# A hybrid decoder step on one core: the turns of the sample's next keys as a stream of their own, and the attention's order planned anew

## The chip, the cores and the metric
One core of a Trainium2 chip. The time is device microseconds of one launch of the whole step, measured from the device's side.

## The reference, cut to what matters
One layer of a decoder for two groups of tokens that share the weights: a prompt of 512 tokens, and a sample group of 8 sequences with 8 new tokens each (64 queries) over a paged cache of 4096 past keys.

```python
a_glu, b_glu, q, k, v, qi, ki, wi, g_c, g_a = split(h @ w_in)
c  = silu(layer_norm(causal_depthwise_conv(a_glu * sigmoid(b_glu))))      # width 31
s  = indexer_scores(qi, wi, ki)                                          # sum_h w relu(qi . ki)
idx = top_k(s)                                                           # 256 keys (sample), 128 (prompt)
o  = softmax(q . k[idx]) @ v[idx]                                        # 8 heads of 64
mix = (sigmoid(g_c) * (c @ w_conv_out) + sigmoid(g_a) * (o @ w_attn_out)) @ w_o
x1 = LN1(alpha * h + mix)
y  = LN2(alpha * x1 + HierMoE(x1) + sigmoid(x1 @ w_pg) * (p @ w_pp))     # 32 experts, 2 of a group of 8
```

For the sample each query gathers its own 256 keys and values from the cache in HBM. The prompt's selection is kept as a mask (an additive bias) over dense logits.

## The kernel before
**One list of jobs.** All matmul work is a list JOBS. TensorE goes through it in order; ScalarE goes through the same list and takes each job's PSUM bank over ("drained"); most jobs share four PSUM banks in a ring (RING = 4). VectorE has its own list VJOBS, GpSimd and SyncE have programs of their own. Engines meet by semaphores only, and each works strictly in its order: an instruction that waits holds up all behind it on that engine.

**The stages.** Entry LayerNorm, indexer scores of the sample, selection of its 256 keys on VectorE (32 rounds of max, index, replace), in parallel the projections; then the attention stage, 348 to 785 us in the profile; then output projections, routing, and the experts, whose weights stream from HBM.

**The attention stage** is the list ATTENTION, which a planner (`merged`) makes of streams before the kernel is built. A string PICKS has one letter for each choice: from which stream comes the next job. The planner's costs only say where jobs of VectorE (conv taps, selection rounds) are slipped between those that answer to TensorE's; the order of TensorE's jobs is the picks, but for two rules: the second of a pair of prompt logits follows the first, and a stream whose next job is `blocked` is passed over.

- *sample*: the 64 queries in 16 groups of four (GQ = 4). For group g: turns `T` of its keys (four jobs of eight transposes, L1179, copied by ScalarE, L1645) for groups 0 to 7; from group 8 on (BY_VECTOR = 8) instead `KQ`, the products of keys and queries on VectorE (L2037, L2042), four a group, nothing on TensorE. Then `QK` logits (L1191, L1209 or L1197 and L1202), with `max` on VectorE (L2167) and `EX` exponentials on ScalarE (L1651); `PT` turn of the weights (L1218); `PV` values (L1227, L1230), which `om` on VectorE scales (L2179); `OS` own rows (L1237).
- *prompt*: index scores `pi` (L1299), then 32 units of `qk` (L1308), `pt` (L1315) and `pv` (L1321), with `unit` and `weigh` on VectorE and the exponentials on ScalarE; the selection rounds (48, L2078 and L2079) are VectorE's. A bias of token tile t must be ready before its units.
- *branch*: the last gates, the LayerNorm of the convolution (`cv`, `cstat`, `croot`, `cnorm`, `cn`, `csilu` L2149), the conv branch `cbP`, `cbS` (L1361), the attention gates `gaP`, `gaS` (L1139). Half of the depthwise convolution is 62 taps on VectorE (L2054) in the same stage; `cv` waits for all of them.
- After the streams comes a fixed ending: the attention branch `abP`, `abS`, `abT`, `oT`.

**Gathers.** GpSimd issues for each group eight indirect DMAs of keys and eight of values, in this order (L1069):

```python
for g in range(NGR):
    if 0 < g <= BY_VECTOR:
        pl.wait_ge(lg_full, g)          # logits of group g - 1 done: its keys are free
    ...                                 # eight gathers of keys of group g
    if g:
        pl.wait_ge(pv_done, g)          # values of group g - 1 done
    ...                                 # eight gathers of values of group g
```

From group 9 on the keys' gathers wait for the products of the group before instead. There is one buffer for keys and one for values: a group's keys can be gathered when the logits of the group before are done, its values when the values product of the group before is done. Turns alternate between two PSUM banks, which `PT` uses too, and `QK` and `PV` share one bank, so `QK` of group g waits for `om` of group g - 1.

**Queries.** SyncE loads the broadcast queries for the products, each at a place between loads of weights that `query_loads` finds from the order of JOBS; a load waits for the product four before.

Of the kernel before, what the change touches and what calls it, by code (L numbers as in the profile page):

```python
# [24 lines left out]
PT = NP // P  # L25
# [16 lines left out]
GQ = 4  # L42
NGR = NS // GQ
# [79 lines left out]
BY_VECTOR = 8  # L123
# [19 lines left out]
def prompt_jobs():  # L143

    jobs = [("ncS",), ("ncP",)] + [("pi", t, h) for t in range(1, PT) for h in range(H)]
    for u in range(0, UNITS + 4, 2):
        jobs += [("qk", u), ("qk", u + 1)] if u < UNITS else []
        jobs += [("pv", u - 4)] if u >= 4 else []
        jobs += [("pt", u - 2), ("pt", u - 1)] if 2 <= u < UNITS + 2 else []
    return jobs  # L150


def branch_jobs():

    jobs = [job for gate in GATES[5:] for job in gate] + [("cv", 0), ("croot", 0)]
    for t in range(NT):
        jobs += ([("cv", t + 1)] if t + 1 < NT else []) + [("cn", t)] + ([("croot", t + 1)] if t + 1 < NT else [])
    jobs += [(kind, g, c) for g in range(4) for c in range(2) for kind in ("cbP", "cbS")]
    jobs += [(kind, g, c) for g in range(4) for c in range(2) for kind in ("gaP", "gaS")]
    return jobs  # L160


def sample_jobs():

    def keys(g):
        return [("KQ" if g >= BY_VECTOR else "T", g, j) for j in range(GQ)] if g < NGR else []
    jobs = keys(0)
    for g in range(NGR):
        turned = keys(g + 1)
        jobs += [("QK", g), ("EX", g), ("PT", g)] + turned[:2] + [("PV", g)] + turned[2:] + [("OS", g)]  # L170
    return jobs


def columns(kind):
# [15 lines left out]

def merged(picks):

    streams = {"sample": sample_jobs(), "prompt": prompt_jobs(), "branch": branch_jobs()}
    jobs, vector_order, ring, slots = [], [], [], []
    pe, act, dve, pool, slow, table, at = 0.0, 0.0, 6.0, 0.5, 0.0, None, 0
    pe_end, act_end, dve_end, landed = {}, {}, {}, {}
# [28 lines left out]
    def gather(g, keys, free):  # L225
        nonlocal pool
        pool = max(pool, free + 0.3)
        for j in range(GQ):
            pool += GATHER
            landed[("T", g, j) if keys else ("PV", g)] = pool + (2.3 if keys else 2.8)  # L230

    def start(job):
        t = released(job)
# [41 lines left out]
        return t  # L275

    def blocked(job):
        if job[0] not in ("pi", "qk", "cbP", "cbS", "abP") or len(slots) < TR:
            return False
        old, following = slots[-TR], slots[1 - TR]  # L280
        if job[0] in ("cbP", "cbS", "abP") and following[0] == "qk" and ("weigh", following[1]) not in dve_end:
            return True
        return old[0] == "qk" and ("pt", old[1]) not in pe_end
# [9 lines left out]
    def put(job):  # L293
# [48 lines left out]
        if kind in ("QK", "PV") and a[0] + 1 < NGR:  # L342
            gather(a[0] + 1, kind == "QK", pe)
    gather(0, True, 0.0)
    gather(0, False, 0.0)
    while any(streams.values()):
        half = bool(jobs) and jobs[-1][0] == "qk" and jobs[-1][1] % 2 == 0
        if streams["prompt"] and blocked(streams["prompt"][0]):
            turn = streams["prompt"].index(("pt", slots[-TR][1]))
            kept = [job for job in streams["prompt"][:turn] if job[0] == "qk"]  # L350
            streams["prompt"][:turn + 1] = [job for job in streams["prompt"][:turn + 1] if job[0] != "qk"] + kept
        free = [k for k in streams if streams[k] and not blocked(streams[k][0])]
        if half and "prompt" in free:
            pick = "prompt"
        else:
            pick, at = picks[at], at + 1
        put(streams[pick].pop(0))
    for job in ENDING:
# [1 line left out]
    return dve, jobs, vector_order + waiting  # L360


HOP, GATHER, TABLE = 0.12, 2.62, 1.28
PICKS = ("pbpbpssppssppsspppbpppsppsppsppsspsbssspbspsssssppsssppsssssssssbsbppssbpssspsppsbpsbsppsbpsssbppssp"
         "ssbpsbbsssppssbsspspspbppsssssppbppspsppspssspbsbppspppspppssppsppsspppppsspssbsppsppbpspppssbpsppsp"
         "bppsbspbsssbsbssssbbsbsbbssbsbssssbsbsbssbsbsssbsssbssbpsssbsbssbsssbsssbssbsbsssbsbsbs")
STREAM = {"s": "sample", "p": "prompt", "b": "branch"}


ATTENTION, VJOBS = merged([STREAM[k] for k in PICKS])[1:]  # L370
WO_ORDER = (0, 3, 1, 2)

# [2083 lines left out]
```

## Time and profile before
| | |
|---|---|
| three runs | 1266.98, 1277.57, 1278.06 us (median 1277.57) |
| profiled execution, its own time | 1269.41 us |
| its span in the trace | 1267.6 us |
| busy: TensorE, VectorE, GpSimd, ScalarE | 1138.5, 744.5, 537.0, 432.1 us |
| mean granted clock of TensorE | 0.954 |

The span is the time from the first to the last instruction of the profiled execution. Times in rows are microseconds from its start. PE is TensorE, DVE VectorE, ACT ScalarE, POOL GpSimd, SP SyncE; L12 is line 12 of the kernel before. In a timeline a row is: start, duration, engine and line, operation, how many in a row; in brackets the idle time of the engine ahead of it and what ended it.

### The profile page before, as it was taken

The numbers are of one execution on the slowest core, as the hardware profiler recorded it, in microseconds if no ns is written. First come the engines' busy times: TensorE is split into PE (matmuls) and PEld (weight loads), VectorE is DVE, ScalarE is ACT, GpSimd is POOL, SyncE is SP. The second block draws the span as 40 slices with busy tenths as digits, with TensorE's granted clock in tenths as the row PEclk, the third lists the DMA queues.
The fourth block names the chain that finished last, engine by engine and source line by source line (L and its number), as shares of the span: only waits on it lengthen the run. The fifth ranks groups of instructions, "written<-read, shape, count | busy, mean of one in ns | idle before, by whom it ended". The sixth has DMA issues, their size and how long they took to land.

```text
span 1267.6 us, 22339 instructions
## 1 busy us (share of the span) xinstructions
PE 1138.5 (90%) x8697; PEld 725.2 (57%) x8697; DVE 744.5 (59%) x1368; ACT 432.1 (34%) x952; POOL 537.0 (42%) x488
## 2 busy tenths in 40 slices
PE   4899999989989767668999999999999999999896
PEld 4525677778654333324556645888885555555442
DVE  1459999999998888787764513444533221111116
ACT  4540124364354366666322212123112222222220
POOL 5000067887876765576677700000003433433310
PEclk9899999989999887778999999999899999998998
DMA  9511222223166565586799853024278999999935
GB/s 323 214 47 42 85 75 70 67 75 104 50 198 172 169 200 166 150 252 202 226 315 299 284 179 105 17 73 161 84 275 323 403 418 411 369 419 415 417 116 194
DMA packets 86200, 258.61 MB, mean 204 GB/s; under 512 B 13311, under 2 KB 45939, under 8 KB 77191
## 3 DMA queue, kind: packets, MB, share of 16 engines
q1 hardware_dynamic: 54816, 168.79, 35.7%
q0 software_dynamic: 28720, 84.98, 21.1%
q10 hardware_dynamic: 2559, 3.40, 0.8%
q8 instruction: 70, 1.15, 0.4%
q14 instruction: 35, 0.29, 0.1%
HBM read 356.78 MB, written 19.05 MB: 296 GB/s over the span
## 4 chain that ended last, share of the span: by engine, by line
PE 45%; DVE 29%; DMA 13%; POOL 7%; issue 4%; ACT 1%; SPq 1%; DVEq 0%; POOLq 0%; ACTq 0%
DMA arena<-in_w_ex 9%; POOL arena L1069 7%; PE ps L1522 7%; DVE arena L1963 6%; DVE arena L1962 6%; DVE arena L1964 6%; PE ps L1139 6%; PE ps L1145 5%; PE ps L1369 4%; PE ps L1544 3%; PE ps L1361 3%; DMA arena<-in_w_in 2%; PE ps L1532 2%; DMA arena<-in_cache_kv,arena 2%; PE ps L1227 2%
## 5 line engine op out<-in xcount | busy, mean ns | idle before, releaser
L1069 POOL DMA_INDIRECT arena<-in_cache_kv,arena x256 | 264.4, 1033 | 118.5 <-issue 73.7
L1139 PE MATMUL ps<-arena 128*128 128x288 f32 (+2 forms) x1120 | 294.4, 424 | 1.1 <-ACT arena L1688 1.1
L1139 PEld LDWEIGHTS ps<-arena 128*128 128x128 f32 (+1 forms) x1120 | 209.6, 189 | 83.3 <-issue 30.3
L1522 PE MATMUL ps<-arena 128*32 128x256 f32 x2144 | 145.4, 388 | 17.1 <-DMA arena<-in_w_ex 16.1
L1095 POOL DMA_INDIRECT scr_ypair<-arena x67 | 66.9, 999 | 165.7 <-ACT arena L1896 161.2
L2359 DVE TENSOR_TENSOR arena<-arena,ps 128x64 f32<-128x64 f32 x67 | 14.9, 222 | 183.3 <-ACT arena L1890 183.3
L1611 ACT ACTIVATE arena<-ps 128x256 f32<-128x256 f32 (+5 forms) x138 | 57.6, 428 | 183.1 <-PE ps L1361 57.2
L1048 POOL TENSOR_TENSOR arena<-arena 128x816 f32<-128x816 f32 x58 | 103.0, 1775 | 17.4 <-ACT arena L1629 10.6
L1145 PE MATMUL ps<-arena 128*128 128x256 f32 (+4 forms) x544 | 105.3, 357 | 0.8 <-ACT arena L1833 0.6
L1145 PEld LDWEIGHTS ps<-arena 128*128 128x128 f32 (+1 forms) x544 | 92.4, 194 | 13.3 <-issue 1.8
L1522 PEld LDWEIGHTS ps<-arena 128*32 128x32 f32 x2144 | 66.3, 111 | 56.8 <-issue 21.9
L1089 POOL DMA_INDIRECT arena<-scr_x,arena x34 | 35.4, 1040 | 145.9 <-DVE arena L2338 135.3
L1962 DVE MAX8 arena<-arena 128x8 f32<-128x2052 f32 x32 | 73.6, 2299 | 1.1
L1544 PE MATMUL ps<-arena 128*32 128x256 f32 x1072 | 72.6, 388 | 1.0 <-issue 0.9
L1963 DVE FIND_INDEX8 arena<-arena 128x8 uint32<-128x2052 f32 x32 | 73.3, 2290 | 0.0
L1964 DVE MATCH_REPLACE8 arena<-arena 128x2052 f32<-128x2052 f32 x32 | 73.0, 2280 | 0.0
L1179 PE MATMUL ps<-arena 128*128 128x128 f32 x256 | 42.5, 320 | 33.6 <-DMA arena<-in_cache_kv,arena 25.7
L1629 ACT ACTIVATE arena<-arena 128x816 f32<-128x816 f32 x60 | 57.0, 970 | 28.6 <-POOL arena L1048 26.3
L1361 PE MATMUL ps<-arena 128*128 128x288 f32 (+1 forms) x192 | 64.1, 483 | 0.0
L1179 PEld LDWEIGHTS ps<-arena 128*128 128x128 f32 x256 | 34.1, 165 | 47.6 <-DMA arena<-in_cache_kv,arena 31.8
L2054 DVE SCALAR_TENSOR_TENSOR arena<-arena 128x512 f32<-128x512 f32 x120 | 56.9, 516 | 2.0
L2037 DVE TENSOR_TENSOR arena<-arena 128x1024 f32<-128x1024 f32 x32 | 39.2, 1224 | 30.4 <-DMA arena<-in_cache_kv,arena 29.4
(342 smaller groups left out, 1649.2 us busy)
## 6 DMA issues: line engine op xcount, KB each, us to landing
arena<-in_w_ex SPq DMA_DIRECT2D x67, 2048.0 KB
arena<-in_w_ex SPq DMA_DIRECT2D x67, 1024.0 KB
arena<-in_w_in SPq DMA_DIRECT2D x20, 1024.0 KB, 5.6
arena<-scr_q SPq DMA_DIRECT2D x32, 256.0 KB, 5.0
arena<-in_cache_kv,arena POOLq DMA_INDIRECT x256, 3.9
arena<-in_w_o SPq DMA_DIRECT2D x4, 1024.0 KB, 5.3
arena<-in_w_pg SPq DMA_DIRECT2D x4, 1024.0 KB, 6.1
arena<-scr_ypair SPq DMA_DIRECT2D x4, 1024.0 KB, 7.9
```

Source lines behind the costliest of these rows:

```text
L1048: nc.gpsimd.tensor_tensor(a[:, 0:CLEN], a[:, 0:CLEN], p[:, 0:CLEN], ALU.add).then_inc(conv_add, 1)
L1069: pl.indirect_dma_start(unit_rows[:, 2 * j + t, half * H * HD:(half + 1) * H * HD], None, I["cache_kv"].rearrange("n (h d) -> (n h) d", h= ...
L1095: pl.indirect_dma_start(S["ypair"].rearrange("n (h d) -> (n h) d", h=4), bass.IndirectOffsetOnAxis(ap=slist[:, q:q + 1], axis=0), ys[q % Y ...
L1139: mm = nc.tensor.matmul(out, w[:, k], hT[:, k, a:b], start=(k == 0), stop=(k == KC - 1))
L1145: mm = nc.tensor.matmul(out, hT[:, k, at:at + rows], w[:, k], start=(k == 0), stop=(k == KC - 1))
L1179: mm = nc.tensor.transpose(PS[4 + m % 2][:, c * P:(c + 1) * P], unit_rows[:, 2 * j + t, c * P:(c + 1) * P], ident)
L1361: mm = nc.tensor.matmul(ps[:, 0:n], w[:, c], src[:, c, at:at + n], start=(c == 0), stop=(c == CC - 1))
L1522: mm = nc.tensor.matmul(PS[2 + q % 2][r:r + BLK, 0:F], xT[:, p % 3, j, 64 * h + BLK * sub:64 * h + BLK * sub + BLK], w[:, 4 * h + j, half, ...
L1544: mm = nc.tensor.matmul(PS[5 + q % 2][BLK * quarter:BLK * quarter + BLK, 0:D // 4], hidT[:, q % 2, c, :], w[:, c, quarter * (D // 4):(quar ...
L1962: step(V.max(m, work))
L1963: V.max_index(idxu[:, r * 8:r * 8 + 8], m, work)
L1964: step(V.match_replace(work, m, work, TAKEN))
```

## The change
The sample stream keeps only logits, exponentials, turn of weights, values and own rows. The turns and products of the keys are a fourth stream, `keys`. What ties them is in `blocked`: keys of group g may come after the logits of group g - 1 (whose buffer they take), and the logits of group g after the last turn or product of its keys. Before, the first two of them stood between `PT` and `PV`, the last two between `PV` and `OS` of the group before, by the stream itself. The planner's landing time of a gather is 3.5 us for keys and values, before 2.3 and 2.8; it enters only where VectorE's jobs are slipped in. PICKS is a new string, of 287 letters as before, so the whole attention order is another one.

```diff
 def sample_jobs():
 
-    def keys(g):
-        return [("KQ" if g >= BY_VECTOR else "T", g, j) for j in range(GQ)] if g < NGR else []
-    jobs = keys(0)
+    jobs = []
     for g in range(NGR):
-        turned = keys(g + 1)
-        jobs += [("QK", g), ("EX", g), ("PT", g)] + turned[:2] + [("PV", g)] + turned[2:] + [("OS", g)]
+        jobs += [("QK", g), ("EX", g), ("PT", g), ("PV", g), ("OS", g)]
     return jobs
+
+
+def key_jobs():
+
+    return [("KQ" if g >= BY_VECTOR else "T", g, j) for g in range(NGR) for j in range(GQ)]
...
-    streams = {"sample": sample_jobs(), "prompt": prompt_jobs(), "branch": branch_jobs()}
+    streams = {"sample": sample_jobs(), "prompt": prompt_jobs(), "branch": branch_jobs(), "keys": key_jobs()}
...
-            landed[("T", g, j) if keys else ("PV", g)] = pool + (2.3 if keys else 2.8)
+            landed[("T", g, j) if keys else ("PV", g)] = pool + LANDING
...
     def blocked(job):
+        if job[0] in ("T", "KQ") and job[1]:
+            return ("QK", job[1] - 1) not in pe_end
+        if job[0] == "QK":
+            return ("KQ" if job[1] >= BY_VECTOR else "T", job[1], GQ - 1) not in jobs
...
-HOP, GATHER, TABLE = 0.12, 2.62, 1.28
-PICKS = ("pbpbpssppssppsspppbpppsppsppsppsspsbssspbspsssssppsssppsssssssssbsbppssbpssspsppsbpsbsppsbpsssbppssp"
+HOP, GATHER, LANDING, TABLE = 0.12, 2.62, 3.5, 1.28
+PICKS = ("ppbbkkkpkppppssbssppkkpkkppsssbspppskpkpskkppssppspppskkkskbsspbsppskkkkbpsssbbpsbskkpksbkbpsbpbbpsk"
...
-STREAM = {"s": "sample", "p": "prompt", "b": "branch"}
+STREAM = {"s": "sample", "p": "prompt", "b": "branch", "k": "keys"}
```

The orders of TensorE around groups 1 to 3, written out from both strings (`T2.0` is the first turn of group 2's keys):

```
before: QK1 EX1 pi3.2 gcP3.1 PT1 pi3.3 T2.0 T2.1 PV1 T2.2 T2.3 pi3.4 pi3.5 OS1 QK2 EX2 pi3.6 pi3.7 PT2 T3.0 T3.1 PV2 T3.2 T3.3 OS2 QK3
after:  QK1 EX1 gcS3.0 PT1 pi2.2 pi2.3 pi2.4 PV1 T2.0 pi2.5 T2.1 pi2.6 OS1 T2.2 T2.3 pi2.7 pi3.0 QK2 EX2 pi3.1 pi3.2 PT2 pi3.3 pi3.4 pi3.5 PV2 T3.0 T3.1 T3.2 OS2 T3.3 gcP3.1 QK3
```

## Rows read from the trace of the kernel before
**Rows 1.** Page of the profile, part 2: tenths in 40 slices of the span.
```profile
...
PE   4899999989989767668999999999999999999896
...
PEclk9899999989999887778999999999899999998998
...
```
**Rows 2.** Stretches: busy us and instructions by engine, clock, DMA share.
```profile
...
354.80:572.40 217.60, 162.20 (x1156) 84.78 (x1155) 184.12 (x492) 123.21 (x272) 147.67 (x144) 0.86 0.64 189
...
619.00:737.00 118.00, 115.03 (x833) 73.00 (x836) 62.15 (x84) 29.50 (x53) 82.44 (x82) 1.00 0.86 286
...
```
**Rows 3.** The gather line (L1069): durations, what its engine waited for.
```profile
...
L1069 POOL DMA_INDIRECT arena<-in_cache_kv,arena x256: 940/946/2779, 347.7 to 727.4; - x128
...
  issue: 73.7, 242
  PE ps L1230: 42.5, 13
...
```
**Rows 4.** Timeline of PE, 382 to 610 us: turns L1179, values L1227 and L1230.
```profile
...
384.64 1.09 PE L1179 MATMUL ps<-arena 128*128 128x128 f32 x8
...
424.90 1.97 PE L1179 MATMUL ps<-arena 128*128 128x128 f32 x8 [7.44 <-DMA arena<-in_cache_kv,arena]
...
473.58 1.97 PE L1179 MATMUL ps<-arena 128*128 128x128 f32 x8 [4.86 <-DMA arena<-in_cache_kv,arena]
...
529.33 3.60 PE L1227 MATMUL ps<-arena 128*8 128x512 f32 x16
...
606.85 1.90 PE L1227 MATMUL ps<-arena 128*8 128x512 f32 x16
608.69 1.04 PE L1230 MATMUL ps<-arena 64*8 64x512 f32 x8
...
```
**Rows 5.** Timeline of DVE: first tap, maxima of groups 8 and 10, products.
```profile
...
354.82 0.54 DVE L2052 TENSOR_SCALAR arena<-arena 128x512 f32<-128x512 f32 x1
...
572.39 0.49 DVE L2167 TENSOR_REDUCE arena<-ps 128x1 f32<-128x320 f32 x1 [1.86 <-PE ps L1202]
...
620.90 0.49 DVE L2167 TENSOR_REDUCE arena<-ps 128x1 f32<-128x320 f32 x1 [1.33 <-PE ps L1202]
...
671.45 1.23 DVE L2037 TENSOR_TENSOR arena<-arena 128x1024 f32<-128x1024 f32 x1 [7.30 <-DMA arena<-in_cache_kv,arena]
```
**Rows 6.** Timeline of POOL: first value gathers of groups 1, 5, 6, 7.
```profile
...
385.01 0.94 POOL L1069 DMA_INDIRECT arena<-in_cache_kv,arena  x1 [2.69 <-PE ps L1230]
...
483.76 0.94 POOL L1069 DMA_INDIRECT arena<-in_cache_kv,arena  x1 [5.17 <-PE ps L1230]
...
506.22 1.02 POOL L1069 DMA_INDIRECT arena<-in_cache_kv,arena  x1 [2.60 <-PE ps L1230]
...
534.53 0.94 POOL L1069 DMA_INDIRECT arena<-in_cache_kv,arena  x1 [8.45 <-PE ps L1230]
```
**Rows 7.** Page, part 6: issues, KB each, us to landing.
```profile
...
arena<-in_w_in SPq DMA_DIRECT2D x20, 1024.0 KB, 5.6
...
arena<-in_cache_kv,arena POOLq DMA_INDIRECT x256, 3.9
...
```
**Rows 8.** Groups of DVE by form, 347 to 790 us: round, swish product.
```profile
...
L2078 DVE MAX8 arena<-arena 128x8 f32<-128x512 f32 x16 | 11.1, 693 | 0.4
L2079 DVE MATCH_REPLACE8 arena<-arena 128x512 f32<-128x512 f32 x16 | 10.8, 676 | 0.0
...
L2149 DVE TENSOR_TENSOR arena<-arena 128x512 f32<-128x512 f32 x4 | 2.8, 691 | 0.1
...
```
**Rows 9.** Timeline of PE, 610 to 745 us: moved jobs, last own rows.
```profile
...
612.19 1.09 PE L1321 MATMUL ps<-arena 128*64 128x128 f32 x16
613.21 0.66 PE L1315 MATMUL ps<-arena 128*128 128x128 f32 x4
...
623.03 2.11 PE L1361 MATMUL ps<-arena 128*128 128x288 f32 x8
...
743.80 1.07 PE L1237 MATMUL ps<-arena 128*64 128x512 f32 x2
...
```

More of the change, by code:

```diff
@@ L360, in merged @@
     return dve, jobs, vector_order + waiting
-HOP, GATHER, TABLE = 0.12, 2.62, 1.28
-PICKS = ("pbpbpssppssppsspppbpppsppsppsppsspsbssspbspsssssppsssppsssssssssbsbppssbpssspsppsbpsbsppsbpsssbppssp"
-         "ssbpsbbsssppssbsspspspbppsssssppbppspsppspssspbsbppspppspppssppsppsspppppsspssbsppsppbpspppssbpsppsp"
-         "bppsbspbsssbsbssssbbsbsbbssbsbssssbsbsbssbsbsssbsssbssbpsssbsbssbsssbsssbssbsbsssbsbsbs")
-STREAM = {"s": "sample", "p": "prompt", "b": "branch"}
+HOP, GATHER, LANDING, TABLE = 0.12, 2.62, 3.5, 1.28
+PICKS = ("ppbbkkkpkppppssbssppkkpkkppsssbspppskpkpskkppssppspppskkkskbsspbsppskkkkbpsssbbpsbskkpksbkbpsbpbbpsk"
+         "ksppkspppppksppsppsbppbbskkpskpppkpppsspspskpkppbkbspppkbsppsskpkpbpspppskppspppkpppsppkpskpbpspskpk"
+         "bppbsspspkkbspbkpsbbkbsbsskbsbskkkbbsbbbssbsbkkskbskbssbkksbksbskbsskkbsbkksbbsssbsbsbs")
+STREAM = {"s": "sample", "p": "prompt", "b": "branch", "k": "keys"}
 ATTENTION, VJOBS = merged([STREAM[k] for k in PICKS])[1:]
```

## The prediction
> **What bounds the kernel now.** I read the busy shares first, then the stretches, then the waits of each engine inside the attention stage (350 to 745 us), the only stage whose order changes. On the page TensorE looks bound nearly everywhere, but its digits fall to 6 to 8 between the twelfth and the eighteenth slice, and its granted clock falls with them [rows 1]. The stretches split the stage in two [rows 2]. From 354.8 to 572.4 TensorE is busy 162.2 of 217.6 us, VectorE 184.1 and GpSimd 147.7, and the clock is 0.86. From 619 to 737 TensorE is busy 115.0 of 118.0 us at clock 1.00: there it is the bound, and a shorter wait elsewhere buys nothing.
>
> What holds the first part? GpSimd waits 42.5 us in 13 places for the last matmul of a group's values [rows 3]. Its queue is keys, values, keys, values, and the value gathers of group g+1 wait for the values product of group g. That product comes late because TensorE stands before it at turns of the next keys, whose gather has barely been issued: 7.44, 4.10 and 4.86 us in groups 2, 3 and 4 (the first and the last in [rows 4]). So GpSimd and TensorE wait for each other, by an order that the program chose. But VectorE is a second limit in the same part. From its first convolution tap at 354.82 to the maximum of group 8 at 572.39 it stands idle for semaphores only 22.9 us, in ten waits of over 0.5 us (1.57, 1.19, 0.57, 0.58, 3.03, 1.81, 2.07, 5.13, 5.14, 1.86; the last is in [rows 5]). So 217.6 - 22.9 = 194.7 us are its instructions and the steps between them. Whatever GpSimd wins, group 8 can't come earlier than this queue allows.
>
> **The change, part by part.** No instruction is added or removed: 316 jobs stay 316, the vector queue keeps 323 entries, and each engine runs the same matmuls, copies and gathers. Only the places move. I worked the new order out by writing the picks out job by job.
>
> (1) Turns ahead of the values. Before, two of the four turns (or products, from group 8 on) of the next keys stand between logits and values in every group from 0 to 14. After, the count is 0 in groups 0 to 4, then 3, 2, 3, 2, 2, 3, 1, 2, 3, 4. From group 7 on these are products of VectorE and cost TensorE nothing. So the edit does its work in five groups. In those the values product no longer stands behind a gather of the next keys, and the five waits of GpSimd for it go: 2.69 + 1.82 + 2.59 + 3.98 + 5.17 = 16.3 us (the first and the last in [rows 6]). I walked the first groups with row prices (gather issues 1.25 us apart, 0.95 and a step of 73.7/242 = 0.30, so 10 for eight [rows 3]; 3.9 to landing [rows 7]; turns 1.1 each, values 1.9 + 1.0 [rows 4]): in each of the five the values product ends before the next key gathers are issued, by 1 to 5 us. That is thin cover. Where it fails, the wait is back at 1 to 3 us. In groups 5 and 6, where three and two turns still stand ahead, my walk gives waits of 5 and 4 us, against 2.60 and 8.45 now [rows 6].
>
> (2) What is late next is VectorE. Its new queue has one selection round and one swish product more ahead of the maximum of group 8: 0.69 + 0.68 and the steps between, 1.5, and 0.7, so 2.2 us [rows 8]. With no idle at all that maximum would start at 354.8 + 194.7 + 2.2 = 551.7, 20.7 us earlier than now. Idle stays, though. The keys of group 1 can't be issued before those of group 0 are through, so some 2.5 us of wait before the first maxima remain; the values of groups 5 to 7 remain behind turns, and the four waits there cost 14.2 of the 22.9 us. Between 3 us (my walk without any friction) and 20 (nothing won) I take half of what there is, 11: the maximum of group 8 at 562.7, 9.7 us earlier.
>
> (3) Groups 8 and 9. The 2.2 us of vector work that came ahead are missing behind, so 12 us are won by the maximum of group 10; against that the first product of group 9 now stands directly behind the maximum of group 8. Its gather is issued only after the logits of group 8 and lands 2.5 + 3.9 = 6.4 us later, two issues and a landing [rows 3, 7]. The summed weights, the bias and unit 22 are queued behind that wait. Since VectorE comes to it late I price it at 1.5 us, between 0 and 6.4. Left: 10.5 us.
>
> (4) Work moved behind group 10's logits, where TensorE is the bound. One conv-branch product (2.0), two turns of the prompt's weights (0.66 each) and one prompt value product (1.1) stood ahead of these logits and now stand behind: 4.4 us more in the saturated part [rows 9]. Gain left: 6.1. Of the 3.0 us that TensorE isn't busy from 619 to 737 [rows 2] one may go: 7.
>
> (5) At nothing: the other selection rounds and the conv taps, which only change neighbours in a full queue; the broadcast loads of queries on SyncE, of which one moves ahead of the load of the last conv weights (that load's first user comes 31 jobs after its slot is free, before 23, so it has more cover; without it a load of some 5.6 us would show [rows 7]); the table loads of ScalarE, 34 changes of table in both orders. The ending (13 jobs) is the same, and all behind 785 us only shifts.
>
> Beside (1) stands a rule. Gather issues take 0.94 us at least and up to 2.78 [rows 3]; their mean is 147.67/144 = 1.025 where VectorE is busy 85%, and 82.44/82 = 1.005 where it is busy 53% [rows 2]. The Trainium skill (SBUF — State Buffer, "SBUF: two separate sides") says that GpSimd and some VectorE instructions share ports under an exclusive lock, and that a DMA issued by GpSimd can starve for its descriptors meanwhile. It speaks against packing gathers beside vector work; by the rows the packing would cost 0.02 us a gather, 3 us at most in all, on an engine with slack, so the sum stays.
>
> **The sum.** 16.3 us of GpSimd waits are removed, of which 9.7 arrive at group 8, 10.5 at group 10 and 7 at the end. Against the profiled execution: 1269.4 - 7 = 1262.4. That execution lies 8.2 us below the median of the three runs (1266.98, 1277.57, 1278.06), which spread by 11 us with nothing changed. Taken from the median, 1277.6 - 7 = 1270.6, and I forecast 1270.
>
> **The rivals.** *A, the clock comes back too.* A values product takes 3.60 us in the slow stretches and 1.90 in the fast ones [rows 4], and the low clock follows TensorE's waits of 4 to 7 us, three of which this order takes away. If they go and nothing takes their place, the chain logits, exponentials, values gets shorter where VectorE waits for it; VectorE then idles only the 3 us of my walk, the maximum of group 8 comes at 554.7, 17.7 us earlier, and by the steps of (3) and (4) 17.7 + 2.2 - 1.5 - 4.4 = 14, with the 3.0 us of TensorE's later idle time out too 17: 1260. The Trainium skill (TensorE: Matmul & The Clock Gate, "HAM oscillation — how this bites in real kernels") says that waits for DMAs throw the engine back to half its clock each time; the trace agrees, with 0.86 granted where those waits are. Against A: TensorE stays idle a quarter of that part, because VectorE feeds it.
>
> *B, the gain is spent before the end.* Turns still stand ahead of values in groups 5 and 6, and the waits move there; 4 to 5 us are won at group 10 and the moved 4.4 us take them back. 1277. For it: TensorE's saturated part got longer by an amount that is certain, while the gain isn't.
>
> *C, slower: products stall VectorE in the second part.* From group 8 on the new queue puts products of the next group ahead of the weights' sum, of conv-branch products and of `om` (the values' scaling). Such products wait for gathers already now, up to 7.30 us [rows 5], but with nothing urgent behind. If in groups 10 to 15 what is queued behind holds TensorE (its ring of four banks full, or own rows waiting for `om`) for 2 us a group, 12 us are lost against 7 won: 1282. It decides from 1.2 us a group on. Against it: between logits and own rows of group 10 TensorE has 17 us of other work, the stall is 11 to 12.
>
> *D, it doesn't do what it says* would be an order in which turns still wait ahead of values; groups 5 to 7 are that, and B contains it.
>
> **How the numbers follow.** Forecast 0.50, A 0.25, B 0.15, C 0.10. One per cent is 12.8 us, about what a measurement of this kernel can tell from no change. Faster by more: most of A and the upper edge of the forecast's own spread, where a median at the lower edge of that spread also puts it, 0.32. Slower by more takes C at a worse price than 12, 0.09. Within: 0.59. The range takes in A with a few microseconds to spare and C's near side: 1255 to 1281.
>
> **What would show it.** Right: in the changed profile GpSimd's waits for the values' last matmul fall from 42.5 to some 25 us, with none over 1 us before the values of groups 1 to 5; TensorE has no wait over 3 us at a turn in groups 1 to 4; the maximum of group 8 starts near 563 and that of group 10 near 610; from there to the last own rows TensorE is busy without a break for some 4 us longer than the 122.9 us between 620.9 and 743.8 [rows 5, 9]. Wrong in size if VectorE's idle until group 8 is below 5 us (A) or above 18 (B); wrong in sign if TensorE waits more than 10 us for VectorE behind group 10 (C).

## The result, and the profile after

| | before | after |
|---|---|---|
| median, us (runs) | 1276.65 (20) | 1266.95 (20) |
| lowest to highest, us | 1266.98 to 1281.46, one at 1915.94 | 1259.62 to 1276.58 |
| profiled execution, us | 1269.41 | 1269.12 |
| its span, us | 1267.6 | 1267.3 |

The ratio is 0.9926, with an interval of 0.9910 to 0.9941: 9.4 us faster by the ratio, 9.7 by the medians. The forecast was a gain of 7 and a median of 1270, with a range of 1255 to 1281.

The two profiled spans are equal all the same, and the first thing to read is why. This is the chain of work that ended last, of the kernel before and of the one after (start, us, what).

```profile
4.88 26.34 DMA arena<-in_w_in
```

```profile
4.90 32.32 DMA arena<-in_w_in
```

The first weights took 6.0 us longer in the profiled execution of after, in a part of the program that the change doesn't touch. It isn't the change that makes them late: the same load took 25.00 us in the kernel *work ahead* below, whose program up to the attention stage is that of after, and 32.22 in *half before*, which has the old order. The first key gather of after starts at 354.1 against 347.7 [rows 3], 6.4 us later. So I count everything in the attention stage from the first key gather, and the ending by itself. All times below are of one profiled execution each, and were read from the rows of the timelines: the start of a group's logits, the starts of VectorE's maxima, the end of the last own rows.

| us behind the first key gather | logits 3 | max 5 | max 8 | max 10 | own rows 15 end | rest of the span |
|---|---|---|---|---|---|---|
| before | 88.9 | 144.5 | 224.7 | 273.2 | 397.2 | 522.8 |
| after | 90.5 | 136.1 | 218.8 | 264.4 | 390.1 | 523.1 |
| won | -1.6 | 8.4 | 5.9 | 8.8 | 7.1 | -0.3 |

The stage became 7.1 us shorter. The logits of group 1 come 4.6 us earlier (40.4 against 45.0), but at those of group 3 nothing is left of it; all of the gain is there at the maximum of group 5. Behind it the number wanders between 5.4 and 9.2. One reason why the logits of group 3 are late lies in the new order: a gate product of the branch, `gcP3.1`, stands directly ahead of them, behind the last turn, and takes 4.36 us at 440.34. No run moves it.

GpSimd's waits first. Gather line of after (L1075), as [rows 3]: durations, and what its engine waited for.

```profile
L1075 POOL DMA_INDIRECT arena<-in_cache_kv,arena x256: 941/947/2773, 354.1 to 727.1; - x128
...
  issue: 74.3, 244
  PE ps L1236: 30.1, 9
  PE ps L1215: 2.4, 2
```

The waits for the last values matmul fell from 42.5 us in 13 places to 30.1 in 9. Where they stand is in the timeline of POOL in after, as [rows 6]:

```profile
378.02 0.94 POOL L1075 DMA_INDIRECT arena<-in_cache_kv,arena  x1 [0.79 <-PE ps L1215]
...
389.20 0.95 POOL L1075 DMA_INDIRECT arena<-in_cache_kv,arena  x1 [0.30 <-issue]
...
447.80 0.94 POOL L1075 DMA_INDIRECT arena<-in_cache_kv,arena  x1 [1.61 <-PE ps L1215]
...
479.56 0.95 POOL L1075 DMA_INDIRECT arena<-in_cache_kv,arena  x1 [1.16 <-PE ps L1236]
...
506.64 0.94 POOL L1075 DMA_INDIRECT arena<-in_cache_kv,arena  x1 [6.45 <-PE ps L1236]
...
532.94 1.20 POOL L1075 DMA_INDIRECT arena<-in_cache_kv,arena  x1 [6.32 <-PE ps L1236]
...
585.52 0.94 POOL L1075 DMA_INDIRECT arena<-in_cache_kv,arena  x1 [9.61 <-PE ps L1236]
```

From 354.11 to 446.20, 64 gathers for four groups, GpSimd waits once, for 0.79 us; the 0.30 ahead of the other gathers is the step between two issues. Its value gathers of groups 1 to 4 wait for nothing (389.20 is the first), those of group 5 for 1.16; the waits of groups 6, 7 and 9 are left. An engine that never waits is a candidate for the bound of that part. The groups of POOL in the two windows (busy us, mean ns of one, idle before) show how its line runs there; first 354.0 to 446.5 of after, then 446.5 to 572.0:

```profile
L1075 POOL DMA_INDIRECT arena<-in_cache_kv,arena x64 | 72.4, 1131 | 21.9 <-issue 18.9 <-ACT arena L1778 2.2 <-PE ps L1215 0.8
```

```profile
L1075 POOL DMA_INDIRECT arena<-in_cache_kv,arena x86 | 86.4, 1004 | 40.5 <-issue 24.7 <-PE ps L1236 14.2 <-PE ps L1215 1.6
```

The first 64 gathers take 1.13 us each and a step of 0.30: 1.43, not the 1.25 of my walk. Of before, 347.5 to 444.6, the same view has

```profile
L1069 POOL DMA_INDIRECT arena<-in_cache_kv,arena x64 | 71.5, 1117 | 27.6 <-issue 18.3 <-PE ps L1230 7.1 <-ACT arena L1772 2.2
```

so they were as slow there. (The first gather of all takes 2.77 us in both kernels, which is 0.03 of each mean.) The 7.1 us of waits are gone from the line, but 0.8 of another wait and 1.5 of longer issues and steps came, and it ends 92.1 us behind its start, 96.9 before: the gain is 4.8.

Timeline of PE in after: turns (L1185), values (L1233, L1236), last own rows, as [rows 4, 9].

```profile
382.76 1.90 PE L1233 MATMUL ps<-arena 128*8 128x512 f32 x16 [0.64 <-ACT arena L1665]
384.59 1.04 PE L1236 MATMUL ps<-arena 64*8 64x512 f32 x8
...
386.19 1.09 PE L1185 MATMUL ps<-arena 128*128 128x128 f32 x8
...
414.95 1.09 PE L1185 MATMUL ps<-arena 128*128 128x128 f32 x8 [2.01 <-DMA arena<-in_cache_kv,arena]
...
434.77 1.97 PE L1185 MATMUL ps<-arena 128*128 128x128 f32 x8 [1.99 <-DMA arena<-in_cache_kv,arena]
...
495.05 1.97 PE L1185 MATMUL ps<-arena 128*128 128x128 f32 x8 [4.47 <-DMA arena<-in_cache_kv,arena]
...
743.17 1.07 PE L1243 MATMUL ps<-arena 128*64 128x512 f32 x2
```

The values come first and the turns behind them. The turns' waits for gathers are 2.39 us at most in groups 0 to 4, against 7.44 before [rows 4]; 4.47 stands where turns still are ahead of the values. Timeline of DVE in after, as [rows 5]: first tap, maxima of groups 3, 8 and 10, and the product behind that of 8.

```profile
361.28 0.76 DVE L2058 TENSOR_SCALAR arena<-arena 128x512 f32<-128x512 f32 x2
...
447.64 0.49 DVE L2173 TENSOR_REDUCE arena<-ps 128x1 f32<-128x320 f32 x1 [5.11 <-PE ps L1215]
...
572.87 0.48 DVE L2173 TENSOR_REDUCE arena<-ps 128x1 f32<-128x320 f32 x1
...
573.87 1.23 DVE L2043 TENSOR_TENSOR arena<-arena 128x1024 f32<-128x1024 f32 x1
...
618.53 0.48 DVE L2173 TENSOR_REDUCE arena<-ps 128x1 f32<-128x320 f32 x1
```

Ahead of the maximum of group 8 VectorE's waits sum to 15.2 us (1.03, 1.44, 2.51, 5.11, 1.08, 4.00), 22.9 before. The longest is for the logits of group 3. Stretches of after, as [rows 2], and tenths, as [rows 1]:

```profile
354.80:572.40 217.60, 173.64 (x1196) 91.03 (x1194) 191.64 (x505) 129.12 (x283) 157.40 (x150) 0.88 0.66 195
...
619.00:737.00 118.00, 116.85 (x799) 74.48 (x800) 60.94 (x83) 31.53 (x58) 79.93 (x80) 1.00 0.85 282
```

```profile
PE   4799999989988787778999999999999999999896
...
PEclk9799999989989897888999999999899999998998
```

The clock in the first stretch went from 0.86 to 0.88 only. As the stage of after starts 6.4 us later, these bounds take in other work there; from the first tap to the maximum of group 8 (361.26 to 572.87, before 354.82 to 572.39) the clock is 0.88 against 0.86 too, and TensorE is busy 167.21 of 211.61 us against 162.17 of 217.57.

### The profile page after: what moved, and what is told of

Read it like the earlier page. It is cut to its first block, busy times and chain, and to the rows that moved or that the text cites. A ratio compares the mean times of both kernels' runs of the same rounds, so it can differ in the third digit from the quotient of the medians.

```text
span 1267.3 us, 22339 instructions
## 1 busy us (share of the span) xinstructions
PE 1144.6 (90%) x8697; PEld 724.8 (57%) x8697; DVE 743.7 (59%) x1368; ACT 432.4 (34%) x952; POOL 540.0 (43%) x488
## 3 DMA queue, kind: packets, MB, share of 16 engines
q1 hardware_dynamic: 54816, 168.79, 35.5%
## 4 chain that ended last, share of the span: by engine, by line
PE 45%; DVE 28%; DMA 14%; POOL 6%; issue 3%; ACT 3%; SPq 1%; POOLq 0%; DVEq 0%; ACTq 0%
DMA arena<-in_w_ex 9%; PE ps L1528 7%; POOL arena L1075 6%; DVE arena L1969 6%; DVE arena L1968 6%; DVE arena L1970 6%; PE ps L1145 5%; PE ps L1151 5%; PE ps L1375 4%; PE ps L1367 4%; PE ps L1550 3%; DMA arena<-in_w_in 3%; PE ps L1538 2%; DMA arena<-in_cache_kv,arena 2%; PE ps L1233 2%
## 5 line engine op out<-in xcount | busy, mean ns | idle before, releaser
L1075 POOL DMA_INDIRECT arena<-in_cache_kv,arena x256 | 267.1, 1043 | 109.1 <-issue 74.3
L1528 PE MATMUL ps<-arena 128*32 128x256 f32 x2144 | 146.3, 390 | 16.1 <-DMA arena<-in_w_ex 15.2
L1151 PEld LDWEIGHTS ps<-arena 128*128 128x128 f32 (+1 forms) x544 | 91.6, 192 | 13.4 <-issue 1.8
L1185 PE MATMUL ps<-arena 128*128 128x128 f32 x256 | 40.9, 311 | 25.1 <-DMA arena<-in_cache_kv,arena 17.8
L2043 DVE TENSOR_TENSOR arena<-arena 128x1024 f32<-128x1024 f32 x32 | 39.1, 1222 | 35.9 <-issue 18.3
L1375 PE MATMUL ps<-arena 128*128 128x256 f32 x256 | 55.9, 380 | 0.8 <-DVE arena L2124 0.8
```

The costliest lines, as they stand in the source:

```text
L1075: pl.indirect_dma_start(unit_rows[:, 2 * j + t, half * H * HD:(half + 1) * H * HD], None, I["cache_kv"].rearrange("n (h d) -> (n h) d", h= ...
L1151: mm = nc.tensor.matmul(out, hT[:, k, at:at + rows], w[:, k], start=(k == 0), stop=(k == KC - 1))
L1375: mm = nc.tensor.matmul(ps[0:rows, 0:GW], mixT[:, k, at:at + rows], w[:, k], start=(k == 0), stop=(k == KC - 1))
L1528: mm = nc.tensor.matmul(PS[2 + q % 2][r:r + BLK, 0:F], xT[:, p % 3, j, 64 * h + BLK * sub:64 * h + BLK * sub + BLK], w[:, 4 * h + j, half, ...
```

## The experiments

Every ratio is to executions of the kernel before that were made beside the kernel in question; their medians lay between 1274.2 and 1276.7 us, so the medians of the table differ by 1 to 2 us from what the ratios say. The next table holds all of them, in the measure of the stage table; the runs of a kernel are in brackets.

| kernel | logits 3 | max 5 | max 8 | own rows 15 end | median, us | ratio, interval |
|---|---|---|---|---|---|---|
| before | 88.9 | 144.5 | 224.7 | 397.2 | 1276.65 (20) | |
| after | 90.5 | 136.1 | 218.8 | 390.1 | 1266.95 (20) | 0.9926, 0.9910 to 0.9941 |
| turns behind | 89.0 | 147.6 | 225.6 | 402.3 | 1278.22 (12) | 1.0036, 1.0004 to 1.0067 |
| turns ahead | 96.0 | 152.8 | 236.3 | 403.5 | 1284.32 (12) | 1.0064, 1.0035 to 1.0094 |
| landing | 88.0 | 133.2 | 216.7 | 387.3 | 1265.30 (8) | 0.9924, 0.9888 to 0.9959 |
| work ahead | 89.0 | 134.5 | 218.1 | 392.0 | 1266.56 (12) | 0.9949, 0.9917 to 0.9982 |
| none between | 89.1 | 145.3 | 223.6 | 401.7 | 1275.90 (12) | 1.0020, 0.9986 to 1.0054 |
| light before | 85.5 | 138.9 | 218.0 | 391.6 | 1274.65 (12) | 0.9972, 0.9940 to 1.0003 |
| light after | 82.5 | 127.6 | 210.8 | 382.2 | 1257.76 (6) | 0.9873, 0.9825 to 0.9921 |
| values early | 88.3 | 133.9 | 217.7 | 387.7 | 1264.77 (12) | 0.9926, 0.9901 to 0.9952 |
| half after | 80.1 | 128.8 | 207.8 | 373.7 | 1242.93 (6) | 0.9743, 0.9703 to 0.9784 |
| half before | 83.0 | 141.6 | 215.6 | 383.0 | 1254.66 (6) | 0.9830, 0.9789 to 0.9872 |
| half first | 80.1 | 128.7 | 211.6 | 383.2 | 1257.38 (6) | 0.9862, 0.9822 to 0.9901 |
| half and light | 77.1 | 122.2 | 201.1 | 366.9 | 1242.12 (6) | 0.9746, 0.9709 to 0.9783 |

Four profiles of nearly the same order (after, landing, work ahead, values early) end the stage at 387.3 to 392.0, mean 389.3. So a single profile tells the stage to some 2 us, and the 7.1 of the profiles and the 9.4 of the runs don't contradict each other.

**Turns behind.** The kernel before, with its order otherwise as it was and all four turns behind the values in groups 0 to 4.

```
-        jobs += [("QK", g), ("EX", g), ("PT", g)] + turned[:2] + [("PV", g)] + turned[2:] + [("OS", g)]
+        jobs += [("QK", g), ("EX", g), ("PT", g)] + turned[:2 if g >= 5 else 0] + [("PV", g)] + turned[2 if g >= 5 else 0:] + [("OS", g)]
```

> The kernel before with one part of the change alone: in groups 0 to 4 all four turns of the next keys stand behind the values product; the letters of the order are the old ones. Theory (the turns ahead of the values in five groups are what the change removes, VectorE is the second limit): GpSimd's waits before the values of groups 1 to 5 fall from 16.3 us to under 5, the maximum of group 8 comes 7 to 10 us earlier, and as no work is moved behind group 10 the kernel is faster by 7 to 11 us (ratio 0.992 to 0.995). Rival (the gain lies in the new order as a whole, the turns are only a part of it): less than 3 us.

It was no faster; my theory missed. GpSimd's waits before the value gathers of groups 1 to 3 went, and others came in their place: 3.09 us before the keys of group 2, 2.95 before the values of group 4, 5.74 before the keys of group 5 and 3.41 before its values. Timeline of PE in this kernel, where they come from:

```profile
450.62 0.63 PE L1330 MATMUL ps<-arena 128*128 128x128 f32 x4 [2.95 <-DVE arena L2054]
...
459.92 1.07 PE L1179 MATMUL ps<-arena 128*128 128x128 f32 x8 [1.10 <-ACT arena L1645]
...
462.57 3.87 PE L1179 MATMUL ps<-arena 128*128 128x128 f32 x16 [1.59 <-ACT arena L1645]
```

The product `cv` of the branch (L1330) stands ahead of the values of group 3, as it does in the kernel before, and waits for VectorE's taps, 2.95 us here and 1.22 there; then the turns wait for ScalarE's copies of turned keys (L1645). The new order has `cv` behind those values. To move the turns and leave the other streams where they were is not the change.

**None between.** That kernel, with the jobs `cv` 0, `qk` 0 to 3, `croot` 0 and `pt` 0 behind the values of group 3 and two turns of group 4, so that no wait for VectorE lies ahead of those values.

```
+for job in [("cv", 0), ("qk", 0), ("qk", 1), ("qk", 2), ("qk", 3), ("croot", 0), ("pt", 0)]:
+    moved(ATTENTION, job, ("T", 4, 2))
```

> The first experiment again (old letters, turns of groups 0 to 4 behind the values), and besides the seven jobs between the turn of the weights and the values of group 3, the first of which waits for VectorE's conv taps, stand behind two turns of group 4's keys. Theory (the first experiment won nothing because other jobs that wait for VectorE and ScalarE still stood ahead of the values and of the next logits, so the order has to be free of both): the values of group 3 end 3 us earlier than there and the kernel is 2 to 5 us faster than there, ratio 0.999 to 1.002. Rival (where the values stand is no matter in the old order, something else paces it): no difference, 1.003 to 1.004.

The values of group 3 end 5.5 us earlier (100.9 against 106.4), but the maximum of group 5 only 2.3 and the stage 0.6. By the medians it lies 2.3 us below the kernel of the experiment before, at the near edge of the theory's 2 to 5, and the intervals overlap, so this doesn't decide between theory and rival. What it shows is that these jobs alone aren't what the old order lacks: it is no faster than before.

**Turns ahead.** The kernel after, with the first two turns of the next group put directly ahead of the values in groups 0 to 4.

```
+for g in range(5):
+    for j in range(2):
+        moved(ATTENTION, ("T", g + 1, j), ("PV", g))
```

> The changed kernel with the first two turns of the next keys put directly ahead of the values product again in groups 0 to 4, all else as in the changed order. Theory: GpSimd's five waits are back at 10 us or more in sum, TensorE waits 3 to 7 us at turns, and 6 us or more of the 9.7 us are lost (ratio to before 0.997 or more). Rival (new order as a whole): 3 us at most are lost, ratio 0.992 to 0.995.

It costs 17 us beside after, 13.4 of them in the stage, 16.7 already at the maximum of group 5. Timeline of POOL in this kernel, first value gathers of groups 2 and 4:

```profile
418.12 0.94 POOL L1086 DMA_INDIRECT arena<-in_cache_kv,arena  x1 [4.09 <-PE ps L1247]
...
472.77 0.94 POOL L1086 DMA_INDIRECT arena<-in_cache_kv,arena  x1 [6.56 <-PE ps L1247]
```

The waits that the change took away are back, 21.9 us before the values of groups 1 to 5 against 16.3 in the kernel before. So the place of the turns is necessary for the gain, and the first experiment says that it isn't sufficient: the rest of the order has to be planned for it.

**Landing.** The kernel after with the planner's old landing times, 2.3 and 2.8 us; 65 of VectorE's 323 entries change places, TensorE's order is the same.

```
-            landed[("T", g, j) if keys else ("PV", g)] = pool + LANDING
+            landed[("T", g, j) if keys else ("PV", g)] = pool + (2.3 if keys else 2.8)
```

> The changed kernel with the planner's old landing times (2.3 and 2.8 us): TensorE's order is the same job for job, VectorE's taps and rounds are slipped in at other places (65 of 323 entries move). Theory: neighbours in a full queue cost nothing, within 2 us of the changed kernel (ratio 0.991 to 0.995). Rival (the planner's landing time places the maxima better and this is a good part of the gain): 4 us or more are lost, ratio over 0.9955.

The same time as after. The landing times, and the places of VectorE's work that hang on them, bring nothing and cost nothing. The rest of VectorE's new order comes with the new PICKS and wasn't tested by itself.

**Work ahead.** The kernel after with the prompt value product and the conv-branch product of step (4) back ahead of the logits of group 10.

```
+moved(ATTENTION, ("pv", 28), ("OS", 9))
+moved(ATTENTION, ("cbP", 1, 0), ("OS", 9))
+moved(VJOBS, ("cbP", 1, 0), ("max", 10))
```

> The changed kernel with one prompt value product and one conv-branch product (3.1 us of TensorE) back ahead of the own rows of group 9, so ahead of group 10's logits; its vector product stands ahead of that maximum too. Theory (VectorE paces up to group 10, TensorE behind it, so work moved across that line counts in full): 2 to 3 us faster than the changed kernel, ratio 0.990 to 0.991, logits of group 10 not later by more than 1 us. Rival (TensorE paces already ahead of group 10): the logits of group 10 come 3 us later and nothing is won, ratio 0.9926.

Nothing came back: the logits of group 10 came 2.9 us later (265.3), where the rival had 3, their maximum 4.1 (268.5) and the last own rows 1.9. By the ratio (0.9949) it is 2.9 us slower than after, by the medians 0.4 faster, and the intervals overlap. What is moved ahead delays what it is put ahead of, as the rival has it.

**Values early.** The kernel after with the turns behind the values in groups 5 and 6 too, and the values of group 8 directly behind their weights' turn.

```
+for job in [("T", 6, 0), ("T", 6, 1), ("T", 6, 2)]:
+    moved(ATTENTION, job, ("pv", 2))
+for job in [("T", 7, 0), ("T", 7, 1)]:
+    moved(ATTENTION, job, ("T", 7, 2))
+moved(ATTENTION, ("PV", 8), ("qk", 22))
```

> The changed kernel with the turns also behind the values in groups 5 and 6, and the values of group 8 directly behind its turned weights: the three places where GpSimd still waits long (6.4, 6.3 and 9.6 us). Theory (VectorE paces to group 8, TensorE after it): these waits fall under 3 us each, yet the kernel wins 3 us at most, ratio 0.990 to 0.993. Rival (GpSimd's waits pace): 6 us or more are won, ratio 0.988 or less.

The time stayed, but the experiment did only a part of what it was made for. The three waits were to fall under 3 us each and fell from 6.45, 6.32 and 9.61 to 5.02, 5.28 and 3.53; with other waits that came, GpSimd's waits for TensorE are some 4 us less in sum. And with the turns gone from between exponentials and weights, TensorE waits 10.4 us for the exponentials there, where after has 2.8. So no gain came of the 6.1 us less in group 9; what the waits of groups 6 and 7 cost stays open.

**Light before, light after.** Both kernels with 60 of 62 convolution taps on 64 of the 512 prompt positions; part of the convolution is left out.

```
+                if w:
+                    out, src = (out[0][:, 0:64], out[1]), (src[0][:, 0:64], src[1])
```

> The kernel before with VectorE relieved: 60 of its 62 conv taps work on 64 of 512 prompt positions (the rest of those channels' convolution is left out), about 28 us less work in the first part, same instructions and waits. Theory (in the old order GpSimd and TensorE wait for each other, VectorE is only a second limit): 3 to 8 us faster than the kernel before. Rival (VectorE alone paces the old order): 15 us or more.

> The changed kernel with the same relief of VectorE (60 of 62 conv taps on 64 of 512 prompt positions). Theory (after the change VectorE's queue is the first limit up to group 8): more is won than with the old order, 8 to 15 us against the changed kernel, ratio to before 0.981 to 0.986. Rival (the loop of gathers, turns, logits and values paces both): 4 us at most are won, ratio 0.9895 or more.

In the stage the relief wins 5.6 us in the old order, as expected, and 7.9 in the new one, at the lower edge of the 8 to 15 (the ratio, 0.9873, misses its range by 0.0013). I took this for VectorE's share at first. The groups of POOL in the light kernel after, 353.5 to 438.5, show another way to read it:

```profile
L1075 POOL DMA_INDIRECT arena<-in_cache_kv,arena x64 | 63.7, 995 | 23.2 <-issue 18.9 <-ACT arena L1778 2.2 <-PE ps L1215 2.1
```

The same 64 gathers take 0.995 us in place of 1.131, so lighter taps also shorten GpSimd's line, by 8.7 us, and VectorE waits longer for it (timeline of DVE, maximum of group 3):

```profile
439.37 0.49 DVE L2175 TENSOR_REDUCE arena<-ps 128x1 f32<-128x320 f32 x1 [8.59 <-PE ps L1215]
```

Two causes were mixed in one edit, and the next four kernels were made to part them.

**Half after, half before.** From group 1 on only the first of the two blocks of keys and values is gathered; the other keeps the rows of group 0, so these kernels compute with other keys and values.

```
-                for t in range(2):
+                for t in range(2 if g == 0 else 1):
```

> This kernel is the changed one, but from group 1 on only the first of the two blocks of keys and of values is gathered anew; the second block keeps the rows of group 0, so the output is that of other keys and values. GpSimd issues 136 gathers in place of 256, and each group's keys and values are there 5 us (four issues of 1.25 us) earlier; no other engine loses an instruction. Theory (VectorE paces the groups up to 8, TensorE those behind): GpSimd's share in the pace is small, so halving it wins 0 to 8 us beside the changed kernel, ratio 0.986 to 0.993 to the kernel before; the last own rows end 0 to 8 us earlier beside the first gather than in the changed kernel. Rival (GpSimd's issues and the gathers' landing still pace the first part): 15 us or more, about 2 us in each of eight groups, ratio below 0.981.

> The same relief of GpSimd in the kernel before. There TensorE stands at the turns of the next keys for their gather (waits of 4 to 7 us in groups 2 to 4) and the values behind them. Theory (what the change removes is this mutual wait): with half the issues those waits shrink in this order too, and halving wins at least as much as in the changed order, 5 to 12 us, ratio 0.990 to 0.996; the two orders come within 3 us of each other beside e9. Rival (the old order is slow for another reason, such as the place of VectorE's work or of the other two streams): halving wins under 3 us here, ratio above 0.998, and the distance to e9 stays 8 us or more.

GpSimd's share is large in both orders: 16.4 and 14.2 us in the stage. The theory of both expectations fell, in the first kernel for the rival's. The second shows that the distance of the two orders stays, 9.3 us in the stage and 11.7 by the medians, though the gathers are now early. Timeline of PE in the old order with half the gathers:

```profile
423.40 1.16 PE L1179 MATMUL ps<-arena 128*128 128x128 f32 x8 [1.33 <-DMA arena<-in_cache_kv,arena]
...
456.10 1.94 PE L1179 MATMUL ps<-arena 128*128 128x128 f32 x8 [5.49 <-ACT arena L1645]
...
476.78 1.11 PE L1179 MATMUL ps<-arena 128*128 128x128 f32 x4 [2.50 <-ACT arena L1659]
...
481.50 1.94 PE L1179 MATMUL ps<-arena 128*128 128x128 f32 x8 [2.98 <-ACT arena L1645]
```

Where TensorE waited 7.44 us for a gather it waits 1.33, but at the turns of groups 4 and 5 it waits 5.49, 2.50 and 2.98 us for ScalarE (copies of turned keys, L1645, and of turned weights, L1659). So these turns wait for two things, and the gather only came last. That this is why the old order stays behind isn't shown: with half the gathers the turns of the new order wait for ScalarE as well, 16.1 us from 354 to 573 against 21.5 in the old one, only behind the values in groups 0 to 4.

**Half first.** Gathers halved in groups 1 to 3 only.

```
-                for t in range(2):
+                for t in range(1 if 0 < g < 4 else 2):
```

> This kernel is the changed one, but in groups 1 to 3 alone only the first of the two blocks of keys and values is gathered anew; the second block keeps the rows of group 0, so the output is that of other keys and values. Groups 4 to 15 gather all. Theory G (in the changed kernel GpSimd itself paces the first four groups: 64 gathers from 354.1 to 446.2 us with 0.5 us of waits among them, 1.13 us each and a step of 0.30): the logits of group 3 stand 90.5 us behind the first gather there and 80.1 with all gathers halved, so here they come at 79 to 83, and of the 16.4 us that halving everywhere wins at the last own rows some 8 to 10 are won here. The ending's shorter loads don't come (9 us of that kernel's gain), so the ratio is 0.983 to 0.987. Theory V (VectorE is what is late next there, as the prediction has it): its queue to group 8 is unchanged, so at most the 5.1 us of its wait before the maximum of group 3 are won, and the rest of its queue holds group 8: 0 to 4 us at the last own rows, ratio 0.989 or more.

The logits of group 3 came at 80.1, as theory G had them, VectorE's wait of 5.11 us for them is gone (timeline of DVE below), and 6.9 us arrive at the end of the stage: between the two, nearer to G (8 to 10) than to V (0 to 4), with the ratio inside G's range.

```profile
438.32 0.95 DVE L2060 SCALAR_TENSOR_TENSOR arena<-arena 128x512 f32<-128x512 f32 x2
439.30 0.49 DVE L2173 TENSOR_REDUCE arena<-ps 128x1 f32<-128x320 f32 x1
```

**Half and light.** Gathers halved from group 1 on, and the light taps; it leaves out what both leave out.

> Both reliefs together in the changed kernel: gathers halved from group 1 on, and 60 of 62 convolution taps on 64 of the 512 prompt positions, which takes some 28 us of work off VectorE in its first 90 us. It leaves out part of the convolution and reads other keys and values. Theory G (the lighter taps helped the changed kernel because the gathers issued beside a tap take 1.13 us in place of 0.99, and VectorE itself had slack): with GpSimd's line already half as long nothing is left for the taps to win, so the last own rows end within 3 us of those of the kernel with halved gathers (373.7 us behind the first gather), ratio 0.971 to 0.976. Theory V (VectorE's queue paces the first part, from group 4 on at least): the taps' relief wins as much as it did alone, 7 us or more, below 367, ratio 0.969 or less.

By the ratio theory G is right (0.9746 against 0.9743), by the stage theory V: the last own rows end at 366.9, 6.8 us earlier. The ending is what hides it, 519.4 us against 514.1. Endings can't be compared between kernels that compute other numbers: the weights' queue moved 165.65 MB here and 168.79 with half the gathers alone, so other weights are fetched, and the two light kernels have endings of 533.5 and 526.1. I go by the stage, with one profile for each kernel: with GpSimd out of the way VectorE holds the first groups, for another 6 to 7 us.

## Why the prediction was right, and where its steps weren't

The forecast was 7 us; 7.1 were won in the stage and 9.4 by the runs. The direction and the waits that went were as forecast. That the sum came out so close is luck: step (2) promised 3.8 us too much, and steps (3) and (4) took 2.1 and 1.7 too little credit. Of the signs, GpSimd's waits fell to 30.1 us and not to 25, and TensorE's last part became 1.7 us longer and not 4; counted from the first gather the maxima of groups 8 and 10 were to come at 215.3 and 262.3 and came at 218.8 and 264.4.

*Step (1), turns ahead of the values.* The waits of groups 1 to 5, 16.3 us, went but for 1.16. That they are needed for the gain is shown from one side (turns ahead: 17 us lost); that they don't make it by themselves from the other (turns behind: nothing won). I counted one wait at these turns; half before showed the second, for ScalarE's copies. Groups 6 and 7, where I had 5 and 4 us, have 6.45 and 6.32, and 9.61 in group 9 I hadn't seen, so the sum is 30.1 where I had some 25; values early cut the wait of group 9 by 6.1 us and won nothing.

*Step (2), what is late next,* is the step that failed. I named VectorE, and priced gathers at 1.25 us apart. They are 1.43 apart in the first four groups, 64 x 0.18 = 11.5 us more than my walk gave GpSimd's line (1.8 of them are the first gather's). That line, and not VectorE alone, bounds these groups: half first, which leaves out 24 of the 64 gathers, won 6.9 us. VectorE is next behind it (another 6.8, half and light). So the maximum of group 8 came 5.9 us earlier, not 9.7, and VectorE's idle time ahead of it was 15.2, not 11. VectorE's own work up to there was sized rightly: 211.6 less 15.2 is 196.4, against 194.7 before and 2.2 more in the forecast.

*The term beside (1), the shared port,* was mis-sized. I took 1.025 against 1.005 us, means over whole stretches, and wrote 3 us at most. Taken gather by gather in after, the 38 beside which VectorE did nothing took 0.95 us in the mean, the 23 beside selection rounds alone 0.95, the 28 beside convolution taps alone 1.14, and the 36 beside products alone (L2043, L2048) 1.16. With the taps at 64 positions the first 64 gathers fell from 1.131 to 0.995 us, 8.7 us in all. The Trainium skill (SBUF — State Buffer, "SBUF: two separate sides") speaks of an exclusive lock between GpSimd and some VectorE instructions. The durations fit it, though no run here shows the lock itself; which instructions stand beside the gathers decides the price. It fell on both orders alike, so it isn't a cost of the change but a limit to its gain.

*Step (3)* had 0.8 us more at the maximum of group 10 than at that of group 8, and 2.9 came: 8.8 in all, against 10.5. The product directly behind the maximum of group 8 waits for nothing (573.87), where I had 1.5.

*Step (4)* charged 4.4 us for work moved behind group 10's logits, less one. From the maximum of group 10 to the last own rows TensorE has 124.6 us where it had 122.9, so 1.7 of net 3.4; in work ahead the moved jobs cost as much on the other side, as far as one profile tells.

*Step (5)* held as far as it was tested: landing shows nothing for the places that the landing times decide. The query loads and ScalarE's tables weren't tested.

*The rivals.* A: the clock came back only from 0.86 to 0.88, and TensorE is still idle a fifth of that part (173.64 of 217.60 busy). B: the waits before the values of groups 6 and 7 are 12.8 us in sum where they were 11.1, and didn't spend the gain. C: products wait for gathers in after too, but TensorE is busy 116.85 of 118.00 us behind group 10, so nothing urgent stood behind them.

What stays open is what else the new order brings, since its turns alone win nothing in the old one. A rival that no experiment takes by itself is TensorE's wait for the exponentials ahead of the weights' turn: from the first gather to the maximum of group 8 it is 10.8 us in before, 10.8 in turns behind and 10.9 in half before, but 2.8 in after and 3.3 in half after. Against it as the whole cause: values early has 10.4, 7.7 of them in group 5, and the time of after. Open too is why the order of before, with its turns moved, gives its waits back one group later, beyond the waits named in the first experiment. And the 16.4 us of half after are 6.9 from groups 1 to 3; the other 9.5 come behind group 7, where VectorE's products wait 2.0 us for gathers in place of 17.5; they weren't parted further.

## What to carry to other kernels

A wait that is removed is worth only what the line behind it can use: price the freed engine's own line with the durations of that very stretch, not with a mean over the stage, before naming what is late next. Moving the job that stands in the way may win nothing while the rest of the order is planned for its old place: try the move alone and in the new order before naming it the cause. An edit meant to relieve one engine may also shorten another's instructions: look at the durations of the neighbours before reading its time.

## What the runs showed of the hardware

Issues of indirect gathers on GpSimd take 0.95 us while VectorE is idle or in selection rounds, 1.14 beside taps of 512 positions and 1.16 beside the products of keys and queries (means in after); beside taps of 64 positions they take 0.95 again (19 gathers in light after). The first weight load of the program took from 25.00 to 32.44 us in the profiled executions of kernels that are the same up to there, which alone makes spans of single executions differ by 6 us and more.
